# Routing of an expert-choice mixture of experts: one expert per partition, two threshold bits a round, 16-wide one-hot tables

## What is computed

```python
def _ec_moe(h, w_router, w_e_gate, w_e_up, w_e_down):
    bsz, t, _ = h.shape
    cap = EC_FACTOR * t // N_EXPERTS          # 32 of 256, 256 of 2048
    logits = jnp.einsum('btd,de->bte', h, w_router).astype(jnp.float32)
    aff = jax.nn.softmax(logits, axis=-1)
    gate, idx = lax.top_k(jnp.swapaxes(aff, 1, 2), cap)
    xs = h[bidx, idx]
    a = jnp.einsum('becd,edf->becf', xs, w_e_gate)
    u = jnp.einsum('becd,edf->becf', xs, w_e_up)
    y = jnp.einsum('becf,efd->becd', jax.nn.silu(a) * u, w_e_down)
    y = y * gate[..., None].astype(h.dtype)
    return jnp.zeros_like(h).at[bidx, idx].add(y)
```

## Time and profile before

| | us |
|---|---|
| median of three runs | 2967.73 |
| profiled execution | 2954.8 |
| its span, first to last instruction | 2953.1 |
| routing after the router's last logits | 1321.9 to 1516.8 |
| hand-over to the first expert matmul | to 1541.4 |
| the sixteen experts | to 2880.7 |
| final norm and stores | to 2953.1 |

### The profile page before, as it was taken

How to read it: one execution, slowest core, us unless ns; L and a number is a source line. 1 busy time by engine, 2 the same in 40 slices (tenths; PEclk the granted TensorE clock), 3 DMA queues, 4 the chain that set the end, 5 groups by cost and what they waited for, 6 DMA issues and landing times.

```text
span 2953.1 us, 45518 instructions
## 1 busy us (share of the span) xinstructions
PE 2599.7 (88%) x16633; PEld 2273.3 (77%) x16633; DVE 1691.8 (57%) x3353; ACT 1174.8 (40%) x1912; POOL 408.5 (14%) x426
## 2 busy tenths in 40 slices
PE   5679999999978899981459999999999999999990
PEld 2668788786855676760249999999999999999990
DVE  0657869495964544325765555555555555555543
ACT  3645454535332333320014444444444444444443
POOL 1020101001000111100011111221121112221100
PEclk9889999999988889885559999999999999999995
DMA  6875565656454344120035565655566565655537
GB/s 207 317 255 177 194 236 175 230 183 204 171 187 154 120 144 152 65 95 0 0 101 167 183 188 179 184 175 160 171 188 188 176 187 177 185 161 170 175 116 279
DMA packets 297627, 500.22 MB, mean 169 GB/s; under 512 B 14142, under 2 KB 251291, under 8 KB 281658
## 3 DMA queue, kind: packets, MB, share of 16 engines
q1 hardware_dynamic: 275258, 376.96, 38.0%
q0 software_dynamic: 22272, 121.94, 14.0%
HBM read 401.98 MB, written 96.88 MB: 169 GB/s over the span
## 4 chain that ended last, share of the span: by engine, by line
PE 80%; DVE 6%; DMA 2%; ACT 2%; issue 2%; DVEq 0%; POOL 0%; POOLq 0%; SPq 0%; ACTq 0%
PE bank L1157 22%; PE bank L1159 21%; PE bank L1158 21%; PE bank L1516 2%; PE bank L1275 2%; PE bank L1503 2%; PE bank L1337 1%; PE bank L1524 1%; DVE work_out L1781 1%; PE bank L1314 1%; PE bank L1403 1%; PE bank L1302 1%; PE bank L1368 1%; PE bank L1394 1%; DMA work_exp<-x_rows 1%
## 5 line engine op out<-in xcount | busy, mean ns | idle before, releaser
L1157 PE MATMUL bank<-act_hl_exp,hl_exp 128*128 128x288 f32 x3072 | 919.2, 299 | 3.9 <-DVE hl_exp L2071 3.9
L1158 PE MATMUL bank<-act_hl_exp,hl_exp 128*128 128x288 f32 x3072 | 907.4, 295 | 0.0
L1159 PE MATMUL bank<-act_hl_exp,hl_exp 128*128 128x288 f32 x3072 | 904.2, 294 | 0.0
L1157 PEld LDWEIGHTS bank<-act_hl_exp,hl_exp 128*128 128x128 f32 x3072 | 576.6, 188 | 6.8 <-DVE hl_exp L2071 4.0
L1159 PEld LDWEIGHTS bank<-act_hl_exp,hl_exp 128*128 128x128 f32 x3072 | 579.6, 189 | 0.0
L1158 PEld LDWEIGHTS bank<-act_hl_exp,hl_exp 128*128 128x128 f32 x3072 | 578.0, 188 | 0.0
L2071 DVE TENSOR_TENSOR hl_exp<-work_exp,hl_exp 128x1024 fp32r<-128x1024 f32 x192 | 235.3, 1225 | 280.5 <-ACT hl_exp L914 280.4
L2071 DVE TENSOR_TENSOR hl_exp<-raw_exp,hl_exp 128x1024 fp32r<-128x1024 f32 x192 | 233.6, 1225 | 229.7 <-ACT hl_exp L914 229.7
L1734 DVE SCALAR_TENSOR_TENSOR work_proj<-work_proj,wcv 128x392 f32<-128x392 f32 (+11 forms) x600 | 343.1, 642 | 0.0
L914 ACT ACTIVATE hl_exp<-work_exp 128x1024 fp32r<-128x1024 f32 x192 | 203.2, 1058 | 268.6 <-PE bank L1159 268.6
L914 ACT ACTIVATE hl_exp<-raw_exp 128x1024 fp32r<-128x1024 f32 x192 | 200.2, 1052 | 166.9 <-PE bank L1159 139.6
(11 more groups left out here) (257 smaller groups left out, 3861.0 us busy)
## 6 DMA issues: line engine op xcount, KB each, us to landing
hl_proj<-park_w POOLq DMA_DIRECT2D x80, 1024.0 KB, 5.5
raw_exp<-in_w_e_gate_dram SPq DMA_DIRECT2D x32, 1024.0 KB, 5.2
raw_exp<-in_w_e_up_dram SPq DMA_DIRECT2D x32, 1024.0 KB, 5.2
work_exp<-in_w_e_gate_dram SPq DMA_DIRECT2D x32, 1024.0 KB
work_exp<-in_w_e_up_dram SPq DMA_DIRECT2D x32, 1024.0 KB
raw_exp<-in_w_e_down_dram SPq DMA_DIRECT2D x32, 1024.0 KB, 6.2
work_exp<-in_w_e_down_dram SPq DMA_DIRECT2D x32, 1024.0 KB
park_w<-hl_proj SPq DMA_DIRECT2D x10, 2048.0 KB, 12.6
```

The source lines that it names most:

```text
L1157: pe.matmul(out, lh, rh, start=first, stop=False)
L1158: pe.matmul(out, lh, rl, start=False, stop=False)
L1159: return pe.matmul(out, ll, rh, start=False, stop=last_)
```

## The change

Layout. `aff` is transposed on TensorE to `affT`: partition 16 g + e holds expert e and the g-th of each eight tiles; 256 columns of latents (two tiles), 128 of the prompt (in 32 partitions only). Two matrices made by POOL in stage 2, `same_e` and `below_e`, sum over the partitions of one expert, or over those of it that come earlier.

Search. 15 rounds written out. In each VectorE counts for three candidates and two sets by a compare with `accum_out`, TensorE adds over an expert's partitions (6 columns), VectorE counts how many candidates passed, and sets two bits.

Ranks by scans along the free axis, bases by two products. `pos` is transposed back to tokens.

Lists. The latent slot is 16 a + b; for each tile a one-hot table `A4` of a and one `B4` of b, both 16 wide, for all experts at once; ScalarE scales `B4` by the token's number into `Bt4`; TensorE's product over tokens gives 16 x 16 numbers an expert, for eight experts at once (128 x 128, of which the diagonal blocks count: `own_e8`, then `Z`). The prompt has a direct table `ohp` of 32 slots.

Order. The barrier behind the routing goes; POOL waits for `k_tab` and for the store of `aff`. SP issues the first four weight units ahead of its wait for the softmax; ScalarE splits two before it scales the tables; VectorE splits its part ahead of the first `gather_mod`. `gather_T` takes 128 rows in its third piece too; POOL zeroes `xg[:, 2, :]` once.

The diff, cut to its core:

```diff
-        OHR = 6
-        W4 = carve(work5, WORK, [("aff", TE), ("mx", NTILE), ("sm", NTILE), ("t1", TE), ("t2", TE), ("sel", TE), ("eq", TE),
...
+        SEG = ((0, 128), (128, 256), (256, 384))
+        cnt_b = W4["cnt"].bitcast(bf16)
+        A4, B4, Bt4 = (W4[n].bitcast(f16).rearrange("p (t e a) -> p t e a", e=NE, a=16) for n in ("A", "B", "Bt"))
+        ohp = W4["ohp"].bitcast(f16).rearrange("p (t e s) -> p t e s", t=2, e=NE)
...
@@ sync
-            sp.wait_ge(k_v, 5)
...
-            sp.wait_ge(k_af, 16)
-            stage_end(sp, 3)
...
+            expert_units(0, range(4))
+            sp.wait_ge(k_v, 5)
+            sp.dma_start(h2_rows[:, D:D + NE].rearrange("(t p) e -> p t e", p=128),
+                         W4["aff"].rearrange("p (t e) -> p t e", e=NE)).then_inc(k_af, 16)
+            expert_units(0, range(4, NEXP))
+            with sp.Fori(1, NE) as e:
+                expert_units(e, range(NEXP))
@@ scalar
-            stage_end(act, 3)
...
+            ehi(0, 0)
+            ehi(0, 1)
+            for t in range(NL):
+                if t % 4 == 0:
+                    act.wait_ge(k_tab, TAB_L + 2 * (t // 4 + 1))
+                act.activation(Bt4[:, t], B4[:, t], ACT.Copy, scale=lat_id[:, t:t + 1]).then_inc(k_bt, 1)
...
             for k in range(KC):
                 xe_hi(0, k)
-            ehi(0, 0)
-            ehi(0, 1)
@@ gpsimd
-            pool.memset(ones_b[:, :], 1.0).then_inc(s_cst, 1)
-            step()
...
+            def routing_constants():
...
+                chain(pool.memset(same_e[:, :, :], 0.0))
+                chain(pool.memset(below_e[:, :, :], 0.0))
+                for g in range(8):
+                    chain(pool.affine_select(out=same_e[:, :, :], in_=same_e[:, :, :], compare_op=ALU.not_equal,
+                                             fill=1.0, base=-NE * g, pattern=[[0, 8], [-1, NE]], channel_multiplier=1))
...
+                if m == 1:
+                    routing_constants()
             stage_end(pool, 2)
...
-            stage_end(pool, 3)
+            pool.memset(xg[:, 2, :], 0.0).then_inc(k_c, 1)
...
+            pool.wait_ge(k_c, N_CONST + 1)
+            pool.wait_ge(k_af, 16)
+            pool.wait_ge(k_tab, TAB_IL)
             gather(0, 1)
@@ tensor
-            mb = W4["mb"].bitcast(bf16)
-            with pe.Fori(0, 30) as i:
+            pe.wait_ge(k_v, 5)
+            for g in range(2):
+                pe.transpose(psum[0][:, 128 * g:128 * g + 128], W4["aff"][:, 2 * NE + 128 * g:2 * NE + 128 * g + 128],
+                             ident[:, :])
+            pe.transpose(psum[0][0:2 * NE, 256:384], W4["aff"][:, 0:2 * NE], ident[:, :]).then_inc(k_T, 1)
+            pe.wait_ge(k_c, N_CONST)
+            for i in range(15):
                 pe.wait_ge(k_m, i + 1)
-                pe.matmul(psum[0][:, 0:TE], ones_b[:, :], mb, start=True, stop=True).then_inc(k_cnt, 1)
...
+                pe.matmul(psum[1][:, 0:6], same, cnt_b[:, 0:6], start=True, stop=True).then_inc(k_cnt, 1)
...
+            for t in range(NL):
+                pe.wait_ge(k_bt, t + 1)
+                for g in range(2):
+                    last = pe.matmul(psum[3 + g][:, 0:128], A4[:, t, 8 * g:8 * g + 8].rearrange("p e a -> p (e a)"),
+                                     Bt4[:, t, 8 * g:8 * g + 8].rearrange("p e b -> p (e b)"), start=(t == 0),
+                                     stop=(t == NL - 1))
...
-                for t, n in ((0, 128), (1, 128), (2, CAPP)):
-                    last = pe.transpose(psum[4 + k % 2][:, 128 * t:128 * t + n], xg[0:n, t, 128 * k:128 * k + 128],
-                                        ident[0:n, 0:n])
+                for t in range(3):
+                    last = pe.transpose(psum[4 + k % 2][:, 128 * t:128 * t + 128], xg[:, t, 128 * k:128 * k + 128],
+                                        ident[:, :])
@@ vector
+            for i in range(15):
+                b = 28 - 2 * i
+                for s, (a, z) in enumerate(((0, 256), (256, 384))):
+                    for c in range(3):
+                        ins = dve.tensor_scalar(W4["A"][:, 3 * a + (z - a) * c:3 * a + (z - a) * (c + 1)], affT[:, a:z], three[:, s, c:c + 1], 0.0, ALU.is_ge,
+                                                ALU.add, accum_out=cnt_b[:, 3 * s + c:3 * s + c + 1])
+                ins.then_inc(k_m, 1)
+                if b:
+                    link(dve.tensor_scalar(step, step, 2, None, ALU.logical_shift_right))
+                dve.wait_ge(k_cnt, i + 1)
+                link(dve.tensor_tensor(ok.rearrange("p (s c) -> p s c", s=2),
+                                       psum[1][:, 0:6].rearrange("p (s c) -> p s c", s=2),
+                                       W4["kk"].unsqueeze(2).broadcast_to([128, 2, 3]), ALU.is_ge))
+                link(dve.tensor_reduce(W4["need"], ok.rearrange("p (s c) -> p s c", s=2), AX.X, ALU.add))
+                link(dve.tensor_copy(passed, W4["need"]))
+                link(dve.scalar_tensor_tensor(out=cand, in0=passed, scalar=b, in1=cand, op0=ALU.logical_shift_left,
+                                              op1=ALU.bitwise_or))
+                if b:
+                    link(dve.tensor_tensor(three.bitcast(u32), cand.unsqueeze(2).broadcast_to([128, 2, 3]),
+                                           step.unsqueeze(1).broadcast_to([128, 2, 3]), ALU.bitwise_or))
...
+            for t in range(0, NL, 4):
+                for dst, src, io in ((A4, pa, iota_a), (B4, pb, iota_b)):
+                    dve.tensor_tensor(dst[:, t:t + 4].rearrange("p t e a -> p (t e) a"),
+                                      src[:, NE * t:NE * t + 4 * NE].unsqueeze(2).broadcast_to([128, 4 * NE, 16]),
+                                      io[:, :].unsqueeze(1).broadcast_to([128, 4 * NE, 16]), ALU.is_equal)\
+                       .then_inc(k_tab, 1)
...
+            for g in range(2):
+                dve.wait_ge(k_cnt, CNT_IL + g + 1)
+                dve.tensor_scalar(ids[:, 8 * g:8 * g + 8, 0:2],
+                                  psum[6 * g][:, 0:16].rearrange("p (e t) -> p e t", t=2), float(TP), None,
+                                  ALU.add).then_inc(k_tab, 1)
...
+            elo(0, 0)
+            elo(0, 1)
             for k in range(KC):
                 gather_mod(0, k)
-            elo(0, 0)
-            elo(0, 1)
```

More of the change, by code:

```diff
@@ L546, in _, with expert_units @@
             stage_end(sp, 2)
[L548 to L555 removed]
+            def expert_units(e, units):
+                for j in units:
                     s = j % 4
@@ new lines, in _ @@
+            pe.matmul(psum[1][:, 24:28], below, cnt_b[:, 0:4], start=True, stop=True).then_inc(k_cnt, 1)
+            pe.wait_ge(k_m, 18)
+            for g in range(2):
+                pe.transpose(psum[2][:, 128 * g:128 * g + 128], W4["pos"][:, 128 * g:128 * g + 128], ident[:, :])
+            pe.transpose(psum[2][:, 256:256 + 2 * NE], W4["pos"][0:2 * NE, 256:384], ident[0:2 * NE, 0:2 * NE])\
+              .then_inc(k_T, 1)
+            pe.wait_ge(k_tab, TAB_P)
+            for e in range(NE):
+                for t in range(2):
+                    last = pe.matmul(psum[5][0:CAPP, 2 * e:2 * e + 2], ohp[:, t, e, :], pr_id[:, t, :], start=(t == 0),
+                                     stop=(t == 1))
@@ new lines, in _, with count @@
+            dve.memset(cand, 0)
+            for c in range(3):
+                ins = dve.memset(W4["three"].bitcast(u32).rearrange("p (s c) -> p s c", s=2)[:, :, c:c + 1], (c + 1) << 28)
+            link(ins)
+            dve.wait_ge(k_T, 1)
+            dve.tensor_copy(affT[:, 0:256], psum[0][:, 0:256])
+            link(dve.tensor_copy(affT[0:2 * NE, 256:384], psum[0][0:2 * NE, 256:384]))
+            def count(out, op, seg, s, c):
+                return dve.tensor_scalar(out[:, seg[0]:seg[1]], affT[:, seg[0]:seg[1]], W4["cand"][:, s:s + 1], 0.0, op,
+                                         ALU.add, accum_out=cnt_b[:, c:c + 1])
@@ new lines, in scans @@
+            def scans(src):
+                for a, z in SEG:
+                    ins = dve.tensor_tensor_scan(W4["scan"][:, a:z], ones[:, :], W4[src][:, a:z], 0.0, ALU.mult, ALU.add)
+                return ins
+            count(W4["gt"], ALU.is_gt, (0, 256), 0, 0)
+            count(W4["gt"], ALU.is_gt, (256, 384), 1, 1)
+            for q in range(3):
+                ins = count(W4["eq"], ALU.is_equal, SEG[q], q // 2, 2 + q)
+            ins.then_inc(k_m, 1)
+            link(dve.memset(W4["off"], 0.0))
@@ new lines, in _ @@
+            for q, (a, z) in enumerate(SEG):
+                ins = dve.scalar_tensor_tensor(out=W4["eq"][:, a:z], in0=W4["scan"][:, a:z], scalar=lim[:, q:q + 1],
+                                               in1=W4["eq"][:, a:z], op0=ALU.is_le, op1=ALU.mult)
+            link(ins)
+            link(dve.tensor_tensor(W4["sel"], W4["gt"], W4["eq"], ALU.add))
+            with nc.allow_low_precision(reason="counts up to 128 are whole numbers that bfloat16 holds"):
```

(10 more changed lines are left out.)

256 lines of the change are left out of this document (110 added, 146 removed).

## The result

The changed kernel takes 2821.22 us (median of 4 runs, 2819.06 to 2828.3) against 2966.07 (2957.41 to 2970.5) beside it: ratio 0.9519, interval 0.9491 to 0.9547, 144.9 us less. The forecast was 2831.

What follows compares the result with a forecast made beforehand. VectorE's chain was taken to bound the routing, TensorE the experts. Savings of 99.9 (routing), 8.6 (hand-over), 28 (transposes) and 0.3 (start) sum to 136.8 us, taking the median from 2967.7 to 2831 us, range 2807 to 2859.

Steps and rivals of the forecast that it cites:

- What bounds it: Routing is bound by VectorE's chain with nothing covering anything; in the experts only TensorE's own time counts.
- Search: Threshold search in the routing: 15 rounds of 4.05 us, 61 us (42 to 77) against 91.85.
- rival (b): Search compares are cheap, two elements a cycle: rounds of 2.8 to 3.5 us, 8 to 19 more saved, 2818; chance 0.14.
- rival (a): Search compares are dear, sum written by a separate instruction: rounds of 4.6 to 5.1 us, 2843; chance 0.14.
- Setup, ranks, pos: Routing around the search: setup 2.0 us, ranks 9.3 against 13.61, transposing pos 1.3.
- Lists: Routing's row-number lists: table products replace 84.50 us of one-hot compares and products, taking 17.0 us.
- Hand-over: From last list to first expert matmul: 16.0 us against 24.64, 8.6 saved (5 to 10), the gather's part falling to 8.
- rival (d): Hand-over: the gather lands no earlier since loads 5 and 6 replace 1 to 4; 4 less saved, 2835; no separate chance.
- Full height: Expert loop's transposes: full-height pieces save 0.47 us a pair, 60 pairs, 28 us; low bound 20.
- Rival (c): Expert transposes: full height does not remove the gap, 28 us of saving gone, 2859; chance 0.07.
- POOL's constants: Output stage: 45 POOL operations take 16 us, covered by POOL's idle 63.82 us, so cost zero.
- rival (e): Output stage: POOL's constants delay the next splits and TensorE's projection, making the kernel slower, 2988; chance 0.01.

Runs made afterwards that it cites:

- x1: Changed kernel with the old transposes of the third piece, 32 rows into 32 columns instead of 128 into 128: 2848.01 us.
- x2: Kernel before with one edit, the full-height third piece of the transposes, its remaining rows cleared once: 2929.49 us.
- x3: Changed kernel with one bit a search round, thirty rounds of one candidate instead of fifteen of three: 2832.38 us.
- x10: Changed kernel with the unused result of the search's compares written as float16 instead of float32: one run, 2815.41 us.
- x0: Changed kernel run again without any edit: 2819.42 us.
- x9: Changed kernel with weight loads 5 and on held until the gather landed, and VectorE's split of the second unit moved behind the modulated columns: 2811.74 us.
- x4: Changed kernel with SP holding the first expert's weight loads 5 and on until the first gather has landed: 2815.17 us.
- x6: Changed kernel with POOL's 45 constant operations moved behind its last block of stage 2: 2814.96 us.

## Why the prediction was right

2831 was forecast, 2821 measured, inside the range and 10 us from the likeliest. The number is closer than its parts: the saving was put 11.0 us too low in the routing and 4.9 too high in the hand-over, which partly cancel, and that is luck. By steps:

- **What bounds it.** Right: VectorE's chain in the routing, TensorE's own time in the experts (x1, x2).
- **Search**, 61 us forecast, 51.3 measured: the mechanism right, a term mis-sized. The compares were put at 2.7 us a round and take 2.01. The rate was right (one element a cycle, 0.48 and 0.34), but I left out that such operations overlap by 0.08, as the bound from L2052 had it, and added 0.1 for the write of the sum, which is hidden. It is the write as on ScalarE that the earlier trace rows suggested: VectorE does not pay it. Product 0.43 for 0.3, small operations 1.00 for 1.05, with the gap of 0.03 outside a loop that the earlier trace rows gave; by x3 that gap, and not the work on VectorE, is where most of the first 28.9 us lie, which the prediction does not say. A round of 3.42 falls into rival (b)'s span, for a reason (b) did not give: not two elements a cycle (x10), but an accumulation without a price. By the Trainium skill's rule (VectorE: DVE Perf Modes, "Two Vector instructions with no wait between them") a compare with its sum is two instructions; the records agree, 0.48 and 0.09, but the next compare starts with the read, so the 77 us priced from it did not come: rival (a) is out.
- **Setup, ranks, pos**: 2.0 + 9.3 + 1.3 = 12.6 forecast, 1.77 + 9.32 = 11.09 measured (the 9.32 hold the transposing of pos). **Lists**: 17.0 forecast, 17.14 measured, tables at 1.15 us (eight in 9.17): 16-bit operands gave nothing over fp32 for this shape.
- **Hand-over**, 16.0 forecast, 20.9 measured (20.0 in x0): the step that failed is the gather's term, 12.25 scaled to 8 by megabytes; 13.2, and 12.35 in x0, lie outside its bounds of 6.5 and 11. Without any load beside it, it is 8.4 (x9), of which 4.6 are POOL's copy and issues (1409.96 to 1414.56), where I took 1 us as fixed; and 2 MB issued in its midst cost as much as 4 ahead. That is rival (d)'s mechanism, at the size it gave (4 less). The split "under some 8" was not free either: it slowed POOL by 0.9 us net (x4 against x9), a collision that I had not counted.
- **Full height**: 28 forecast, 28.7 measured, 28 in x1 and x2. Rival (c) is out.
- **POOL's constants**: 16 us forecast, 16.6 measured (977.05 to 993.69), the next split at 1042.96, nothing waits; rival (e) is out, and x6 shows no change clear of the noise.
- Of the signs named: rounds of 3.42 for 4.05; a second record, but free; tables and experts as said; POOL's copy 84 us after the logits for 95; ScalarE's splits done by 1340.5.

So the routing saved 11.0 us more than forecast, the hand-over 4.9 less, the experts 0.7 more, and the 0.3 put down for the start has no row of its own: together the 6.5 by which 143.4 exceeds 136.8.

## What to carry to other kernels

Price an operation by the start of the next one, not by its record: ninety compares of 0.48 and 0.34 us with reads of 0.09 cost 0.40 and 0.27 each. Look at the idle time between an engine's own operations before its work: in the search of the kernel before, VectorE was idle for 40 of 92 us, most of it in gaps of 0.15 and 0.48 us of a loop on the device, and written-out rounds left 0.03. In a serial search weigh the fixed part of a round against a candidate's price (here 1.44 against 0.66, by which two bits are the best width). When a preparation is moved ahead, look at what its end releases: here the loads of the next units landed in the midst of the gather that all waited for, and took back most of the gain until they were held.

## What the runs showed of the hardware that I had not expected

- POOL's 128x1024 subtraction stretches VectorE's 2-to-6-element operations from 0.17 to 2.27 us, and VectorE's stretches POOL's copy of 3 columns from 0.19 to 1.00 and the issue of a gather from 0.96 to 1.86; accumulating compares and a reduce beside them keep their length.
- VectorE's read of its accumulator (0.09 us) is hidden behind the next operation.
- Dependent VectorE operations stand 0.15 us apart in the device loop of the kernel before and 0.48 where it turns (row 1333.30), and 0.03 in written-out rounds.
- Transposes of mixed height cost TensorE 0.44 to 0.47 us for each group of six, twice 0.17 of it as plain gaps.
- The same output stage ends 7 us apart in two executions of one kernel (1321.9 and 1328.8).
